# One burst of S5 output products, 256-column value slices, and both heads of a pair side by side

## What is computed

```python
h = rmsnorm(x, norm_w[i]);  proj = h @ w_in[i]
u, s5_gate, z, xbc, dt_raw, q, k, v, att_gate, merge_logits = split(proj)
# A: S5. bu = B_bar u;  s_t = lam_bar * s_{t-1} + bu_t;  y = Re(C s) + d*u;  gelu, GLU, silu gate
# B: SSD (Mamba-2), 16 heads of 64.  y = (C B^T * exp(segsum(a))) @ (x*dt) + ...; gated rmsnorm
# C: sliding-window attention, 16 query heads of 64, 4 kv heads:
s = q @ k.T * 64**-0.5 (masked);  m = max(max(s), sink)
p = exp(s - m) / (sum(exp(s - m)) + exp(sink - m));  o = p @ v
x = x + (sum_b sigmoid(gate_b) * (branch_b @ w_branch_b)) @ w_out
```

## Time and profile before

| | us |
|---|---|
| median of 3 runs | 2083.73 |
| lowest, highest | 2082.57, 2084.92 |
| the profiled execution, its own time | 2086.78 |
| its span, first to last instruction | 2085.1 |
| PE busy | 1996.8 |
| DVE busy | 1555.8 |
| ACT busy | 1044.8 |
| POOL busy | 663.2 |
| granted TensorE clock, mean over the span | 0.99 |

### The profile page before, as it was taken

The page is one execution under the profiler, slowest core; times in us unless marked ns, Lnnn a source line. Parts: engine busy times, 40 slices in busy tenths (PEclk is TensorE's granted clock), DMA queues, the critical chain, the costliest instruction groups (busy, mean ns, idle before and its releaser), DMA issues.

```text
span 2085.1 us, 37174 instructions
## 1 busy us (share of the span) xinstructions
PE 1996.8 (96%) x12460; PEld 1741.5 (84%) x12460; DVE 1555.8 (75%) x2145; ACT 1044.8 (50%) x1334; POOL 663.2 (32%) x816
## 2 busy tenths in 40 slices
PE   4999999999999998999989999999999999989998
PEld 4999999777777798889979999987777777978898
DVE  6758888788888857566567688888888878566655
ACT  5343344667675654333443444447666666443343
POOL 3045656434343000002400665565343330000034
PEclk9999999999999999999999999999999999999999
DMA  6344444444444445665643444444444444456656
GB/s 257 122 168 146 160 146 159 154 165 148 149 162 150 146 171 222 222 233 203 202 147 142 168 155 150 152 155 163 142 156 163 148 148 153 170 222 232 235 191 210
DMA packets 57900, 359.07 MB, mean 172 GB/s; under 512 B 6928, under 2 KB 7440, under 8 KB 18960
## 3 DMA queue, kind: packets, MB, share of 16 engines
q1 hardware_dynamic: 54480, 345.03, 46.8%
q0 software_dynamic: 1600, 7.85, 1.1%
q10 hardware_dynamic: 1696, 4.72, 0.6%
HBM read 340.27 MB, written 19.40 MB: 172 GB/s over the span
## 4 chain that ended last, share of the span: by engine, by line
PE 84%; issue 5%; DVE 4%; POOL 3%; DMA 2%; ACT 2%; DVEq 0%; POOLq 0%; ACTq 0%; SPq 0%
PE mm L1485 13%; PE mm L1486 13%; PE mm L1487 13%; PE mm L1526 12%; PE mm L1528 11%; PE mm L1527 11%; PE bs L1611 2%; PE b L1599 2%; DVE prod L888 1%; DMA raw<-in_stream 1%; POOL ssum L427 1%; PE by L1670 1%; PE b L1661 1%; DVE w_lo L884 1%; PE b L1682 1%
## 5 line engine op out<-in xcount | busy, mean ns | idle before, releaser
L589 ACT ACTIVATE w_hi<-raw 128x2048 fp32r<-128x2048 f32 x299 | 571.9, 1913 | 681.6 <-DMA raw<-in_stream 677.0
L884 DVE TENSOR_TENSOR w_lo<-raw,w_hi 128x2048 fp32r<-128x2048 f32 x299 | 696.9, 2332 | 159.7 <-ACT w_hi L589 152.5
L1485 PE MATMUL mm<-h_lo,w_hi 128*128 128x256 f32 x2240 | 648.5, 290 | 5.7 <-DVE h_lo L888 5.5
L1486 PE MATMUL mm<-h_hi,w_lo 128*128 128x256 f32 x2240 | 635.7, 284 | 0.0
L1487 PE MATMUL mm<-h_hi,w_hi 128*128 128x256 f32 x2240 | 635.6, 284 | 0.0
L1485 PEld LDWEIGHTS mm<-h_lo,w_hi 128*128 128x128 f32 x2240 | 431.8, 193 | 18.9 <-issue 10.8
L1486 PEld LDWEIGHTS mm<-h_hi,w_lo 128*128 128x128 f32 x2240 | 431.8, 193 | 2.2 <-issue 1.0
L1487 PEld LDWEIGHTS mm<-h_hi,w_hi 128*128 128x128 f32 x2240 | 431.5, 193 | 0.0
L1526 PE MATMUL mm<-w_lo,h_hi 128*128 128x512 f32 x768 | 322.8, 420 | 0.8 <-ACT gt L703 0.6
L1528 PE MATMUL mm<-w_hi,h_lo 128*128 128x512 f32 x768 | 303.1, 395 | 0.0
L1527 PE MATMUL mm<-w_hi,h_hi 128*128 128x512 f32 x768 | 302.1, 393 | 0.0
(11 more groups left out here) (276 smaller groups left out, 2897.3 us busy)
## 6 DMA issues: line engine op xcount, KB each, us to landing
raw<-in_stream SPq DMA_DIRECT2D x300, 1024.0 KB, 4.8
gscr<-gt SPq DMA_DIRECT2D x48, 256.0 KB, 5.9
gin<-gscr SPq DMA_DIRECT2D x24, 512.0 KB, 5.7
x_old<-out POOLq DMA_DIRECT2D x2, 2048.0 KB, 9.9
out<-proj ACTq DMA_DIRECT2D x8, 512.0 KB, 6.4
proj<-in_x SPq DMA_DIRECT2D x4, 512.0 KB, 7.1
par<-in_params POOLq DMA_DIRECT2D x2, 759.0 KB, 4.7
cst<-in_consts SPq DMA_DIRECT2D x1, 1029.0 KB, 16.8
```

The lines of the kernel that those rows point to most:

```text
L589: e.activation(w_hi[:, j % RAW, :], raw[:, j % RAW, :], ACT.Copy).then_inc(hi_done, 1)
L884: e.tensor_tensor(w_lo[:, j % RAW, :], raw[:, j % RAW, :], w_hi[:, j % RAW, :].bitcast(F32), ALU.subtract).then_inc(lo_done, 1)
L1485: e.matmul(out, whi, xlo, start=start, stop=False)
L1486: e.matmul(out, wlo, xhi, start=False, stop=False)
```

## The change

It regroups small products and the steps around them:

- **Values.** Pieces 6 and 7 are laid out by rows: each holds eight 128-row slices of all 256 v columns. 96 products of 256 columns take the place of 192 of 128, into the banks `by` and `bs`, and DVE reads both at step 7 (`v_in`).
- **S5 output products.** The four `cs(j)` become one `cs()` of eight matmuls, the four 32-row groups of the array in turn, behind pieces 7 (input stage) and 11 (gate stage). DVE puts the states of all quarters in a new buffer `state`; `prod` has one buffer.
- **Mixer tile.** Both heads have buffers of their own (`ex`, `pr`, halves of `small`), `stt` and `sc` go. PE makes `diff(1)` in block 3, both heads' scores (`a1`) behind block 3, both heads' `ssd_y` behind block 4, both transposes in the middle of block 5, both `a3` behind it. DVE makes `att_scores(0)` behind its `lo` of t = 3 and both `att_sum` behind its `lo` of t = 4. ACT makes both heads' `att_exp` and `att_norm` behind its `hi` of t = 4 and both `pt_out` behind its `hi` of t = 5.

```diff
@@ ACT
-                            if t == 4:
-                                att_exp(1)
-                            if t == 5:
-                                pt_out(1)
                             if s % QUAD == QUAD - 1:
                                 gate(s // QUAD, 0)
                                 gate(s // QUAD, 1)
                             hi(nb, s + LEAD)
...
                             if t == 3:
+                                head_exp(1)
+                            if t == 4:
                                 att_exp(0)
-                                head_exp(1)
+                                att_exp(1)
                                 att_norm(0)
-                            if t == 4:
-                                pt_out(0)
-
+                                att_norm(1)
                                 MA.mark(... "tz")
                                 MA.mark(... "ta")
                             if t == 5:
+                                pt_out(0)
+                                pt_out(1)
                                 W.wait(MV, "yatt")
@@ DVE
-                            if t == 3:
-                                att_scores(0)
...
-                            if t == 4:
-                                att_sum(1)
...
                             lo(nb, s + LEAD)
...
                             if t == 3:
-                                att_sum(0)
                                 st_make(1)
+                                att_scores(0)
                                 att_scores(1)
                             if t == 4:
-                                W.wait(MP, "ys1")
+                                att_sum(0)
+                                att_sum(1)
+                                W.wait(MP, "ys")
@@ PE, values
-                            for k in range(KT):
-                                w, tok = slice(k * P, k * P + P), slice(t * P, t * P + P)
-                                ins = prod3(mm[:, n % 2, tok], h_hi[:, k, tok], h_lo[:, k, tok], ...)
+                            for k in range(BT):
+                                w, tok, kt_ = slice(k * TOK, k * TOK + TOK), slice(t * P, t * P + P), (n - 6) * BT + k
+                                ins = prod3((by, bs)[t][:, 0:TOK], h_hi[:, kt_, tok], h_lo[:, kt_, tok], ...)
@@ PE, S5
-                    def cs(j):
+                    def cs():
+                        W.wait(SGp, "cz11")
+                        W.wait(SV, "y5", 1)
+                        W.wait(SV, "sim3")
                         for r in range(2):
-                            ins = e.matmul(ps_s5[32 * j:32 * j + 32, :], cz[:, j, r, :], prod[:, j % 2, r, :], ...)
+                            for j in range(4):
+                                ins = e.matmul(ps_s5[32 * j:32 * j + 32, :], cz[:, j, r, :], state[:, j, r, :], ...)
@@ PE, mixer
+                                    diff(1)
+                                if q == 2 and t == 5:
+                                    a2(0)
                                     a2(1)
...
                             if t == 3:
-                                ssd_y(0)
-                                a1(0)
-                                diff(1)
+                                a1()
                             if t == 4:
-                                a2(0)
-                                ssd_y(1)
+                                ssd_y()
                             if t == 5:
-                                a3(0)
-                                a3(1)
+                                a3()
```

More of the change, by code:

```diff
@@ L726, in att_exp @@
[L726 to L731, removed]
+                            o = 16 * h
@@ L794, in _ @@
                 W.wait(MV, "end")
-                W.wait(MP, "A3_1")
+                W.wait(MP, "A3")
                 W.wait(SGp, "end")
+                W.wait(MG, "end")
                 for tok in range(2):
@@ L1266, in att_sum @@
-                            MV.mark(e.reciprocal(small[:, 10:12], small[:, 6:8]), f"rden{h}")
+                            W.wait(MA, f"pn1{h}", 1)
+                            MV.mark(e.reciprocal(small[:, o + 10:o + 12], small[:, o + 6:o + 8]), f"rden{h}")
                         for t in range(6):
@@ L1663, in diff @@
                             MP.mark(e.matmul(b6[:, 256:384], m1[:, 2, :], C("tri", P), start=True, stop=True), f"diff{h}")
-                        def ssd_y(h):
-                            W.wait(MV, f"ST{h}")
-                            if not h:
-                                W.wait(MV, "yatt", 1)
-                            rows = slice(64 * h, 64 * h + 64)
-                            e.matmul(ps_ssd[rows, :], xdt[:, 0, h, :], stt_[:, 0:256], start=True, stop=False)
-                            MP.mark(e.matmul(ps_ssd[rows, 128:256], xdt[:, 1, h, :], stt_[:, 256:384], start=False, stop=True), f"ys{h}")
@@ L1673, in a1, with ssd_y @@
-                        def a1(h):
-                            W.wait(MV, f"sc{h ^ 1}", 0 if h else 1)
-                            if not h:
-                                W.wait(MV, "qh")
-                                if c == 0:
-                                    W.wait(MG, "vcur")
-                                    e.wait_ge(k_in, keys)
-                            rows = slice(64 * h, 64 * h + 64)
-                            e.matmul(b7[:, 0:128], qh[rows, 0:P], kcur[rows, 0:P], start=True, stop=True)
-                            MP.mark(e.matmul(b7[:, 128:384], qh[rows, P:TOK], kcur[rows, :], start=True, stop=True), f"A1_{h}")
+                        def ssd_y():
+                            W.wait(MV, "ST1")
+                            W.wait(MV, "yatt", 1)
+                            for q, cols in enumerate((slice(0, 256), slice(128, 256))):
+                                for h in range(2):
+                                    ins = e.matmul(ps_ssd[64 * h:64 * h + 64, cols], xdt[:, q, h, :], ex[:, h, (slice(0, 256), slice(256, 384))[q]],
+                                                   start=q == 0, stop=q == 1)
+                            MP.mark(ins, "ys")
@@ new lines, in a1 @@
+                        def a1():
+                            W.wait(MV, "qh")
+                            if c == 0:
+                                W.wait(MG, "vcur")
+                                e.wait_ge(k_in, keys)
+                            for cols, toks in ((slice(0, 128), slice(0, P)), (slice(128, 384), slice(P, TOK))):
+                                for h in range(2):
+                                    rows = slice(64 * h, 64 * h + 64)
+                                    ins = e.matmul((b7, b5)[h][:, cols], qh[rows, toks], kcur[rows, 0:toks.stop], start=True, stop=True)
+                            MP.mark(ins, "A1")
@@ L1693, in a3 @@
                             W.wait(MV, "yv")
[L1694 to L1696 removed]
+                            for q, cols in enumerate((slice(0, 256), slice(128, 256))):
+                                for h in range(2):
+                                    ins = e.matmul(ps_att[64 * h:64 * h + 64, cols], vcur[:, q, :], pt[:, h, (slice(0, 256), slice(256, 384))[q]],
+                                                   start=q == 0, stop=q == 1)
```

155 lines of the change are left out of this document (68 added, 87 removed).

## The result

The changed kernel takes 2142.74 us (median of 4 runs, 2131.93 to 2152.41), the kernel before 2084.32 (4 runs, 2082.57 to 2086.21): 1.0279 times as long, with a 95% interval of 1.0224 to 1.0333. It is slower by 58 us, where 51 were predicted. The profiled execution of after took 2147.3 us with a span of 2145.6.

What follows compares the result with a forecast made beforehand. PE was taken as the bound by a small margin, with the order on DVE and ACT deciding. Values -8, input stage -24, mixer tiles +58, clock +22 and +3 gave +51 us, 2135; range 2095 to 2165.

Steps and rivals of the forecast that it cites:

- the likeliest case: Whole kernel: the forecast sum holds, 2125 to 2145 us, chance 0.46.
- The chain of the mixer tile: Gate stage: PE waits for DVE and ACT before a2 and a3; 7.2 us a pass, 58 in eight passes.
- The clock: Half-clock stretches of 1.7 us lost behind PE's waits: 13 in the 8 passes, 22 us, plus 3 at G.
- With the clock up: Rival: the clock stays up behind PE's new waits, 2110 us, chance 0.14.
- The rule of the Trainium skill: Rival: each group of matmuls behind a wait starts cold, 24 slow stretches of 1.7 us, 2151 us, chance 0.15.
- Gate stage, other terms: Gate stage: mixer tiles cost 58 us, slow clock there 22 us.
- "Nothing" for the products that go: Gate stage: S5 products removed save nothing, since block 8 waits for ACT's gate read and xT for DVE as before.
- Input stage: S5 output products become one burst of 1.1 us: 3.0 us saved a pass, 24 in eight passes.
- the 1.8 us by which DVE would end behind PE: Input stage: DVE finishes states(3) about 1.8 us behind PE, and the burst waits for exactly that.
- Values: Preparation: fewer value products, bc_silu3 2.0 us earlier, G 4.1 us earlier in each of 2 layers, 8 us saved.
- Four groups don't run at once: Rival: the four 32-row groups run in turn, the burst costs 4.2 us in 16 tiles, 2185 us, chance 0.07.
- DVE arrives in time: Rival: DVE catches up its lag in the gate stage, a pass costs 1.7 us, 2052 or 2070 us, chance 0.14.

Runs made afterwards that it cites:

- x_sum: Changed kernel with both att_exp (ACT) and both att_sum (DVE) moved ahead of the split of t = 4: 2085.44 us, 1.0001 to the kernel before.
- x_pt: Changed kernel with only pt_out of t = 5 moved on ACT, behind the first gate read, ahead of the second and the split: 2110.50 us, 1.0134.
- x_fill: Changed kernel with products nobody reads ahead of a2(0) in both tiles and of a3 in c = 1: 2109.52 us, 1.0122 to the kernel before.
- x_order: Changed kernel with att_scores, att_sum (DVE) and att_exp ahead of the splits, pt_out ahead of the second gate read (ACT): 2040.86 us, 0.9787.
- x_valburst: Kernel before with the S5 burst and the 256-column value slices, without the mixer part: 2067.40 us, 0.9907 to the kernel before.
- x_light: x_order with the input stage's four additions per S5 part on DVE done on 8 of 256 columns only: 2024.40 us, 0.9693.

## Why the prediction was right, and where it was not

- **Side and size.** Slower by 51 was forecast, 58 came. The median of 2142.74 lies in the range of the likeliest case, 2125 to 2145, and in the whole one. That it came out near is in part luck: errors of both signs lie in the sum (the table above).
- **The chain of the mixer tile** was right to tenths in most tiles. In c = 1, from the end of block 9 (432.23) `a2` starts 15.0 us later (13.3 to 15.4 in the eight tiles), forecast 15.15; in c = 0, from 488.37, 13.6, forecast 13.8, and `a3` at 17.5, forecast 18.0. The waits that I gave as 4.9, 2.9 and 3.3 us were 4.5 in the mean (3.3 to 5.4), 2.8 and 3.8 from start to start; in all 89 us, as forecast. `x_sum` and `x_pt` show that both causes named (DVE's `lo` ahead of the sums; gate read and `hi` ahead of `pt_out`) are the causes. `a3` in c = 1 came at 24.8 and not 22.4 (the steps that I listed add up to 22.3, and the 0.65 of c = 0 to 0.7): the half block between ran at half clock.
- **The clock** was mis-sized. I took 13 slow stretches of 1.7 us lost. The gate stage of after has 18, of 3.4 or 6.8 us, 89 us in all, so up to 44 lost against 5 before. What they are worth there is seen in `x_fill`: 28 us, for the 22 in the sum. With the clock up I had priced 2110, and `x_fill` is at 2109.5, but its preparation met a shorter wait for `bz` than that of after, so the tenths are luck. The rule of the Trainium skill (TensorE: Matmul & The Clock Gate, HAM oscillation — how this bites in real kernels), by which every wait starts cold (2151), lies as near to the result as my sum, 8 us off; the trace agrees with it behind all eight waits of `a2` in c = 1 and seven of eight of `a3`, and behind two of the eight waits of 2.8 us.
- **Gate stage, other terms.** 80 was forecast, 68 came. In `x_fill`, where the clock stays up, the stage is 40 us longer than before, for 58. The term that I had wrong is `xT`, on which PE was to wait as before: DVE's second gap is gone, and PE waits 2.7 us for it in `x_fill` and 1.2 in after, in place of 13.3. The two stretches up to `a3` are 4.7 (c = 1) and 0.2 us (c = 0) longer in `x_fill` than before, in the mean of eight; with my 1.6 for the two `diff`s that is 6.4 a pass, 51 in all, and without the 10.6 of `xT` 41, by this estimate, for the 40 of the trace. "Nothing" for the products that go was right: block 8 waits 11.1 us in all for ACT's read, 0.6 before. The shorter PE work of the pairs (26 us in a good order, by `x_order` against `x_valburst`) doesn't show here, where DVE and ACT set `a2` and `a3`.
- **Input stage.** -24 forecast, -17.8 in the trace, -11 for the burst alone. The burst was right (1.07 us, forecast 1.1). The failed step is the 1.8 us by which DVE would end behind PE. I looked at the end of the chain alone; PE meets DVE already at `bu`, up to 2.0 us a pass from start to start, and again at the burst (0.43 above). `x_light` shows that DVE sets the pass.
- **Values.** -8 forecast, +5 in the trace's preparation. The first step that failed is that the rest of DVE's chain "stays" while its idle time goes. DVE in after, ahead of `bc_silu3`,

```profile
98.91 2.29 DVE L880 TENSOR_TENSOR w_lo<-raw,w_hi 128x2048 fp32r<-128x2048 f32 x1 [2.02 <-ACT w_hi L588]
101.12 0.42 DVE L1085 SCALAR_TENSOR_TENSOR proj<-bt,kk 128x256 f32<-128x256 f32 x1
```

The idle time of 1.92 us went, but the `lo` ahead of it starts 1.1 us later than before (82.87 for 81.77), behind a wait of 2.37 us for ACT's half, and DVE idles ahead of the last `lo` as long as before (2.02 for 1.94). So `bc_silu3` starts 0.5 us earlier (101.12 for 101.63) and not 2.0. `G` starts at 101.60 for 104.18, 2.6 us earlier and not 4.1 (the layer itself began 0.5 later), behind a wait of 5.6 us. The second is "Saved: 4.1 x 2 layers", a saving that I didn't follow from `G` to the stage's end. `prep_end` on ACT, behind a `hi` that waits for weights, came 0.3 us earlier (130.42 for 130.70); POOL's chain to `bz` hangs by it, and `bz` met a `lo`.

- **The rivals.** "Four groups don't run at once" is refuted by the row. "DVE arrives in time" fell in this order, and came true in another: 2041 with moved lines. I had the right chain for it and did not ask what it would be with the sums ahead of `lo`.

## What to carry to other kernels

When small products are put together, the steps that feed them must move too: list what the feeding engines do between the last input and the first use, and put the short dependent operations ahead of the long independent ones. Follow a saving to the end of its stage, through every engine that the next stage's first product waits for, before it goes into a sum. Fifteen of the sixteen waits of 3.3 to 5.4 us had two prices here, the wait and the half clock behind it, and they can be told apart with products that nobody reads.

## What the runs showed of the hardware

- Products that nobody reads, put into PE's waits, made the kernel 33 us faster (granted clock 0.964 to 0.988), about 28 of them in the stage where they stand.
- Four 32-row groups, eight matmuls, take 1.07 us together, and 1.09 when each group's two stand behind each other.
- A POOL operation of 1.04 us takes 3.09 when it meets a DVE operation of two inputs, with the same code in one layer or kernel and not in another.
- DVE has 2.9 to 3.5 us of "issue" at the start of each round of a loop, and in some kernels or rounds a second gap of 1.1 to 3.8 us, that comes and goes with changes elsewhere.
